# Opening of a two-layer transformer kernel: the modulation's first weights read in column halves

## The reference

```python
def rms_norm(x, g):
    xf = x.astype(jnp.float32)
    y = xf * lax.rsqrt(jnp.mean(xf * xf, axis=-1, keepdims=True) + EPS)
    return (y * g.astype(jnp.float32)).astype(x.dtype)
...
    c_act = jax.nn.silu(c)
    for l in range(DEPTH):
        mods = jnp.split(c_act @ w_ada[l] + b_ada[l], N_MOD, axis=-1)
        sh1, sc1, gt1, sh2, sc2, gt2, sh3, sc3, gt3 = mods

        h = modulate(rms_norm(x, g_ffn1[l]), sh1, sc1)
        x = x + 0.5 * gt1[:, None, :] * swiglu(h, w1_gu[l], w1_down[l])
```

## Time and profile before

| | us |
|---|---|
| median of 3 runs | 2141.09 (2136.44 to 2141.6) |
| the profiled execution's own time | 2139.85 |
| its span, first to last instruction | 2138.1 |
| PE busy | 2077.5 (97%) |
| DVE busy | 1385.1 (65%) |
| ACT busy | 815.6 (38%) |

### The profile page before, as it was taken

How to read it: one execution, slowest core, us unless ns; L and a number is a source line. 1 busy time by engine, 2 the same in 40 slices (tenths; PEclk the granted TensorE clock), 3 DMA queues, 4 the chain that set the end, 5 groups by cost and what they waited for, 6 DMA issues and landing times.

```text
span 2138.1 us, 30256 instructions
## 1 busy us (share of the span) xinstructions
PE 2077.5 (97%) x12206; PEld 1782.2 (83%) x12206; DVE 1385.1 (65%) x1992; ACT 815.6 (38%) x1178; POOL 50.0 (2%) x62
## 2 busy tenths in 40 slices
PE   7999999999999999999999999999999998999998
PEld 6888888788887777889998988777688887989897
DVE  7766665644324774576886777766565467869595
ACT  4222212412332563443342444566443433424243
POOL 2000000000000000000000000000030000000000
PEclk9999999999999999999999999999999999999999
DMA  9554553232222112222232223301133122323322
GB/s 369 216 192 186 196 193 122 80 117 96 99 91 88 40 58 81 79 99 106 91 118 95 102 99 117 140 21 41 43 116 138 40 79 89 111 86 104 113 98 109
DMA packets 36745, 238.36 MB, mean 111 GB/s; under 512 B 4454, under 2 KB 6758, under 8 KB 8872
## 3 DMA queue, kind: packets, MB, share of 16 engines
q1 hardware_dynamic: 35132, 232.10, 29.7%
q10 hardware_dynamic: 1516, 4.94, 0.6%
HBM read 230.73 MB, written 6.29 MB: 111 GB/s over the span
## 4 chain that ended last, share of the span: by engine, by line
PE 85%; DVE 8%; ACT 4%; issue 2%; POOL 1%; DMA 0%; SPq 0%; DVEq 0%; ACTq 0%; POOLq 0%
PE ps L649 84%; PE ps L1075 1%; ACT w_hi L1502 1%; DVE ada_acc L2386 1%; DVE w_lo L2204 1%; DVE w_lo L2562 1%; POOL x L2157 0%; DMA ada_slot<-in_ada 0%; DVE w_lo L2739 0%; ACT square L1502 0%; ACT pt L1502 0%; DVE act_lo L2261 0%; ACT act_hi L1502 0%; ACT normed L1502 0%; DVE normed L2702 0%
## 5 line engine op out<-in xcount | busy, mean ns | idle before, releaser
L649 PE MATMUL ps<-act_hi,w_hi 128*128 128x512 f32 (+1 forms) x1672 | 617.1, 369 | 12.9 <-DVE w_lo L2562 4.6
L649 PE MATMUL ps<-act_hi,w_lo 128*128 128x512 f32 (+1 forms) x1672 | 607.4, 363 | 0.0
L649 PE MATMUL ps<-act_lo,w_hi 128*128 128x512 f32 (+1 forms) x1672 | 607.2, 363 | 0.0
L1502 ACT ACTIVATE w_hi<-raw 128x2048 fp32r<-128x2048 f32 (+4 forms) x205 | 339.2, 1660 | 312.3 <-PE ps L649 295.5
L649 PEld LDWEIGHTS ps<-act_hi,w_hi 128*128 128x128 f32 x1672 | 317.0, 190 | 69.4 <-issue 9.8
L649 PEld LDWEIGHTS ps<-act_hi,w_lo 128*128 128x128 f32 x1672 | 316.9, 190 | 49.7
L649 PEld LDWEIGHTS ps<-act_lo,w_hi 128*128 128x128 f32 x1672 | 317.2, 190 | 47.1 <-issue 1.0
L2204 DVE TENSOR_TENSOR w_lo<-raw,w_hi 128x2048 fp32r<-128x2048 f32 x102 | 234.0, 2294 | 56.2 <-ACT w_hi L1502 54.5
L649 PE MATMUL ps<-hid_hi,w_hi 128*128 128x512 f32 (+1 forms) x680 | 260.7, 383 | 2.8 <-DVE hid_lo L2729 1.7
L649 PE MATMUL ps<-hid_lo,w_hi 128*128 128x512 f32 (+1 forms) x680 | 259.6, 382 | 0.0
L649 PE MATMUL ps<-hid_hi,w_lo 128*128 128x512 f32 (+1 forms) x680 | 259.5, 382 | 0.0
(11 more groups left out here) (419 smaller groups left out, 3177.0 us busy)
## 6 DMA issues: line engine op xcount, KB each, us to landing
raw<-in_weights SPq DMA_DIRECT2D x176, 1024.0 KB, 4.8
ada_raw<-in_ada SPq DMA_DIRECT2D x30, 1024.0 KB, 4.8
ada_slot<-in_ada SPq DMA_DIRECT2D x6, 1024.0 KB, 14.7
bias_rows<-biasrow SPq DMA_DIRECT2D x8, 320.0 KB, 17.2
x<-in_x SPq DMA_DIRECT2D x1, 2048.0 KB, 8.2
table<-bias_rows ACTq DMA_DIRECT2D x1, 2048.0 KB, 8.9
result<-x SPq DMA_DIRECT2D x7, 256.0 KB, 2.2
kept_x<-x ACTq DMA_DIRECT2D x1, 1536.0 KB, 5.1
```

The costliest lines, as they stand in the source:

```text
L649: return nc.tensor.matmul(out, lhsT, rhs, start=start, stop=stop)
L1502: return nc.scalar.activation(out, in_, func, **kw)
```

## The change

The two groups that the first layer needs (scale 1 and shift 0) are read and summed in **halves of 512 columns**: first the columns of features 0 to 511 of group 1, then of group 0, then the columns of features 512 to 1023 in the same order. Each half is 4 loads of 512 KB in rows of 2048 bytes.

- Weight block 0 is loaded right behind `x`, ahead of the modulation; block 1 between the two halves.
- Of each half, input tiles 0 and 1 (half 0) or tile 0 (half 1) are multiplied on PE straight from the loaded weights, one column at a time (`first_products`). DVE sums the other 6 or 7 tiles of 128 x 512, with the running sum in PSUM and the last step into `ada_acc` (`first_sum_of`); PE adds that over the partitions (`first_columns`).
- The first 4 tiles of `act_hi` and `act_lo` are made from half 0, and PE multiplies blocks 0 and 1 by these 4 tiles (`first_half(0, 0)`, `first_half(1, 0)`) before the other 4 tiles of both. Its order is written out: block 0 half 0, then block 1 half 0, columns of half 1, block 0 half 1, block 1 half 1.
- `keep_warm` is gone from the opening. `w_lo` of block 0 is made by POOL instead of DVE.
- The bias rows are made one by one in banks 0 to 3, and ACT copies three of them before `x` is there.
- `ada_step`, on which SP's `next_ada` waits, is raised by 16 at once, with `negsink`, after the last `act_lo` tile.

```diff
+FIRST_ON_PE = ((0, 1), (0,))
+FIRST_DONE, _at = {}, 0
+for _half in range(2):
+    for _g in (1, 0):
+        _at += 8 - len(FIRST_ON_PE[_half])
+        FIRST_DONE[_half, _g] = _at
...
+        halves_of = [buf[:].rearrange("p u (e n) -> p (u e) n", e=2) for buf in ada_raw]
+        first_slots = {(0, 1): (act_slots[0][:], act_slots[2][:]), (0, 0): halves_of,
+                       (1, 1): (act_slots[1][:], act_slots[3][:]), (1, 0): (y[:, 0:4, :], y[:, 4:8, :])}
...
+            def load_first(half, g):
+                cut = slice(half * (D // 2), half * (D // 2) + D // 2)
+                for part in range(2):
+                    for b in range(2):
+                        at = (4 * g + 2 * part + b) * BLOCK
+                        block = ten["ada"][at:at + BLOCK].rearrange("(p u n) -> p u n", p=P, u=2)
+                        sp.dma_start(first_slots[half, g][part][:, 2 * b:2 * b + 2, :],
+                                     block[:, :, cut]).then_inc(ada_first_in[half, g][part], 16)
...
-            load_first(0)
-            load_first(1)
+            load(0, 0)
+            load_first(0, 1)
             sp.dma_start(ident, ten["consts"][:, 0:P]).then_inc(ident_in, 16)
-            for b in range(2, ADA_FIRST):
-                load_first(b)
-            load(0, 0)
+            load_first(0, 0)
             load(0, 1)
+            load_first(1, 1)
+            load_first(1, 0)
...
+            def first_products(half, g, t):
+
+                pe.wait_ge(ada_first_in[half, g][t // 4], 32)
+                for j in range(4):
+                    mm(first_column(half, g, j), first_slots[half, g][t // 4][:, t % 4, j * P:j * P + P],
+                       c_act[:, t:t + 1], False, False)
+
+            def first_columns(half, g):
+
+                pe.wait_ge(first_step, FIRST_DONE[half, g])
+                for j in range(4):
+                    at = 4 * half + j
+                    last = mm(first_column(half, g, j), ada_acc[g][:, at * P:at * P + P], ones[:, 0:1],
+                              False, j == 3)
+                if (half, g) == (1, 0):
+                    last.then_inc(ada_sum, 2)
+                else:
+                    last.then_inc(first_sum, 1)
+
+            def first_half(k, half):
+
+                pe.wait_ge(block_used, k + 1)
+                for t in range(4 * half, 4 * half + 4):
+                    if t < 6:
+                        pe.wait_ge(second_low if k else first_low, t // 2 + 1)
+                    else:
+                        pe.wait_ge(split_lo, k + 1)
+                    pe.wait_ge(act_ready, t + 1)
+                    for u in range(2):
+                        cut = slice(u * P, u * P + P)
+                        out = ps[:, 2 * k + u, :]
+                        mm(out, w_hi[k][:, t, cut], act_hi[:, t, :], t == 0, False)
+                        mm(out, w_hi[k][:, t, cut], act_lo[:, t, :], False, False)
+                        last = mm(out, w_lo[k][:, t, cut], act_hi[:, t, :], False, t == DT - 1)
+                if half:
+                    last.then_inc(block_done, 1)
...
+            pe.wait_ge(c_ready, 1)
+            for g in (1, 0):
+                begin_columns(0, g)
+                for t in FIRST_ON_PE[0]:
+                    first_products(0, g, t)
             begin_stats()
             pe.wait_ge(sq_ready, DT)
             add_columns(square[0])
             add_columns(square[1], stop=True).then_inc(ms_ready, 1)
-            ada_columns(0)
+            first_columns(0, 1)
             pe.wait_ge(ident_in, 16)
             pe.wait_ge(rinv_ready, 1)
             for i in range(NT):
                 last = mm(ps[:, 5, i * P:i * P + P], rinv[:, i:i + 1].to_broadcast([P, P]), ident)
             last.then_inc(rstd_ready, 1)
             norms[0] += 1
-            keep_warm(4 * WARM)
-            ada_columns(1)
-            keep_warm(5 * WARM)
+            first_columns(0, 0)
+            first_half(0, 0)
+            pe.wait_ge(first_mods, 1)
+            for g in (1, 0):
+                begin_columns(1, g)
+                for t in FIRST_ON_PE[1]:
+                    first_products(1, g, t)
+            first_half(1, 0)
+            first_columns(1, 1)
+            first_columns(1, 0)
+            first_half(0, 1)
+            first_half(1, 1)
...
+            for h in range(3):
+                bias_row(h)
             act.wait_ge(x_in, 16)
-            for t in range(3):
+            for t in range(5):
                 squares(t, x[:, t, :])
-            bias_rows(0)
-            squares(3, x[:, 3, :])
-            bias_rows(1)
-            squares(4, x[:, 4, :])
-            bias_rows(2)
+                bias_row(3 + t)
             squares(5, x[:, 5, :])
-            bias_rows(3)
+            act.wait_ge(raw_in[0], 16)
+            first_hi_half(0)
             squares(6, x[:, 6, :])
             squares(7, x[:, 7, :])
+            first_hi_half(1)
...
+            act.wait_ge(first_mods, 1)
+            prenorm(mods[:, 0:8], 0, 4, after=second_hi)
+            second_hi(3)
             act.wait_ge(mods_ready, 1)
-            prenorm(mods[:, 0:8], after=second_hi)
+            prenorm(mods[:, 0:8], 4, DT)
...
+                pool.wait_ge(first_hi if t < 2 else split_hi, 1)
+                pair = slice(2 * t, 2 * t + 2)
+                nc.gpsimd.tensor_tensor(w_lo[0][:, pair, :], raw[0][:, pair, :],
+                                        w_hi[0][:, pair, :].bitcast(F32),
+                                        ALU.subtract).then_inc(first_low if t < 3 else split_lo, 1)
...
+            def first_sum_of(half, g, ts):
+
+                bank = (2, 5)[g] if half == 0 else 4
+                total = ada_acc[g][:, half * (D // 2):half * (D // 2) + D // 2]
+                order = [t for t in range(DT) if t not in FIRST_ON_PE[half]]
+                for t in ts:
+                    at = FIRST_DONE[half, g] - len(order) + order.index(t)
+                    dve.wait_ge(ada_first_in[half, g][t // 4], 32)
+                    out = total if t == order[-1] else ps[:, bank, :]
+                    tile = first_slots[half, g][t // 4][:, t % 4, :]
+                    if at:
+                        dve.wait_ge(first_step, at)
+                    if t == order[0]:
+                        ins = v.tensor_scalar(out, tile, c_act[:, t:t + 1], None, ALU.mult)
                     else:
-                        dve.wait_ge(ada_step, 2 * b + u)
-                        ins = v.scalar_tensor_tensor(out=acc[:], in0=ada_slots[b][:, u, :],
-                                                     scalar=c_act[:, t:t + 1], in1=acc[:],
-                                                     op0=ALU.mult, op1=ALU.add)
-                    ins.then_inc(ada_step, 1)
-
-            def first_low(u):
-
-                dve.wait_ge(split_hi if u else first_hi, 1)
-                half = slice(4 * u, 4 * u + 4)
-                ins = v.tensor_tensor(w_lo[0][:, half, :], raw[0][:, half, :],
-                                      w_hi[0][:, half, :].bitcast(F32), ALU.subtract)
-                if u == 1:
-                    ins.then_inc(split_lo, 1)
+                        ins = v.scalar_tensor_tensor(out=out, in0=tile, scalar=c_act[:, t:t + 1],
+                                                     in1=ps[:, bank, :], op0=ALU.mult, op1=ALU.add)
+                    ins.then_inc(first_step, 1)
...
-            for b in range(6):
-                ada_first_block(b)
+            on_dve = [[t for t in range(DT) if t not in ts] for ts in FIRST_ON_PE]
+            first_sum_of(0, 1, on_dve[0])
+            dve.wait_ge(brow_copied, 8)
+            first_sum_of(0, 0, on_dve[0][:-2])
             norms[0] += 1
             dve.wait_ge(root_ready, 1)
             v.reciprocal(rinv[:, 0:NT], root[:, 0:NT]).then_inc(rinv_ready, 1)
-            ada_first_block(6)
-            ada_first_block(7)
-            first_low(0)
-            modulation(0, 2)
-            gain(0, 1, "g_ffn1").then_inc(mods_ready, 1)
-            v.tensor_scalar(negsink[:], col("sinks", 0, 16), -1.0, None, ALU.mult)
-            dve.wait_ge(mods_ready, 1)
+            first_sum_of(0, 0, on_dve[0][-2:])
+            link(first_modulation(0, 1))
+            first_gain(0)
             dve.wait_ge(rstd_ready, 1)
-            prenorm(gains[:, 0], mods[:, 0:8], begin=lambda: first_low(1))
+            first_gained(0)
+            first_gained(1)
+            first_modulation(0, 0).then_inc(first_mods, 1)
+            first_gained(2)
+            first_act_low(0)
+            first_gained(3)
+            for t in range(1, 4):
+                first_act_low(t)
+            first_sum_of(1, 1, on_dve[1])
+            first_sum_of(1, 0, on_dve[1][:-2])
+            link(first_modulation(1, 1))
+            first_gain(1)
+            first_sum_of(1, 0, on_dve[1][-2:])
+            first_gained(4)
+            first_gained(5)
+            first_modulation(1, 0).then_inc(mods_ready, 1)
+            first_gained(6)
```

(64 more changed lines are left out.)

44 lines of the change are left out of this document (12 added, 32 removed).

## The result

| | before | after |
|---|---|---|
| median of 5 runs each, us | 2136.45 (2136.24 to 2141.6) | 2152.09 (2147.9 to 2152.55) |
| the profiled execution's own time | 2139.85 | 2151.61 |
| its span | 2138.1 | 2149.8 |
| block 2 starts on PE | 65.4 | 76.9 |
| span behind that | 2072.7 | 2072.9 |

The ratio of the mean times is **1.0061, 95% interval 1.0048 to 1.0074**: the change makes the kernel slower by 0.6%. (The medians lie 0.7% apart, since the five times before fall into two groups, near 2136.4 and near 2141.3, and their median is in the lower one.) The last two rows say where: block 2 starts 11.5 us later, and all behind it lasts as long as before. The forecast had +7.5 us for that start.

A forecast was written before the change was run, and what follows sets the result against it. The prediction took PE's back-to-back products from 49 us on as the bound. Late root and reload move block 2's start from 65.4 to 72.9, +7.5 us on 2139.85: 2147.4 us, range 2139.5 to 2153.

The forecast's parts named there:

- a late root: Opening: PE's one-column products come ahead of the statistics, which end at 29.85 us instead of 26.76.
- a late reload: Before block 2: modulation load issued at 61.4 us behind `negsink`, landing at 66.2; block 2 starts at 72.9 instead of 65.4.
- unseen costs: Opening: PSUM sums, clock of first products and load behind `negsink`, together about -3 to +3 us: 2144.5 to 2151.
- rival 3: Opening loads: 0.5 MiB loads don't overlap, 3.6 us each, over 2166 us; slowed by a quarter only, 2150.5; together 13%.
- 1.16 a head: PE's bias rows in the opening: cost as before, 1.16 us a head, ending near 15.7 us.
- a wait for group 0's load: PE, half 0: group 1's tiles fit until 19.2 us, group 0's start with their load at 20.5.
- The clock between one-column products and waits: PE, opening: upper level from 41.5 us, block 1's 24 products done at 52.5, group 1's columns at 53.5.
- The last stretch: Opening's end: last `act_lo` at 61.3 us, then reload, two sums, a product and `w_lo` until block 2 at 72.9.
- (1): PE, opening: one-column products take 0.119 us at the upper level; block 2 at 65.0, 2139.5 us; 12%.
- (2): Before block 2: with rival 1, the reload is also hidden and block 1's end decides, 61.7; 2136.2 us; 3%.
- (4): Before block 2: load lands by 60 us, block 1's end decides, 69.6 to 71.7; 2144 to 2146 us; 10%.

The follow-up runs named there:

- Experiment 3: Changed kernel with bias rows made again by pairs of heads on two PE row groups: block 2's `silu` 2.4 us sooner, at 85.74 us.
- e5: Changed kernel with the modulation reload released early and products of zeros in PE's waits: 2144.77 us, one execution.
- e10: Changed kernel with one edit, POOL's four subtractions for block 1 waiting for the fourth `act_lo`: 2147.85 us, one execution.
- e1: Changed kernel with `negsink` and its `ada_step` increment moved up behind half 0's shift, so the reload is issued early: 2149.28 us, one execution.
- e4: Changed kernel with half 1's group 1 columns moved to the middle of block 1's first half on PE: 2152.94 us, one execution.
- Experiment 9: Changed kernel with half 0's sums on DVE, early reload, zero products, columns amid, POOL's block 1 subtractions later: 2141.33 us median of 10, ratio 1.0006 to before.
- e6: Changed kernel with bias pairs, earlier squares and root, tiles moved, columns amid, early reload, zero products in PE's waits: 2147.66 us median of 7, ratio 1.004 to before.
- e2: Changed kernel with all tile sums on DVE, none of PE's one-column products of `w_ada`: 2140.43 us, one execution.
- e7: Changed kernel with all tile sums on DVE, the same kernel as e2, timed: 2144.77 us median of 10, ratio 1.0025 to before.

## Why the prediction came out as it did

**Sign and mechanism.** Slower by more than 0.3%, by a late root and a late reload, as forecast. The forecast time, 2147.4 us, is 4.2 below the profiled execution's own 2151.61. That lies inside the whole range (2139.5 to 2153), near its end, and above the 2144.5 to 2151 that the forecast's own unseen costs spanned: neither of the two terms that were missed below stood among these costs, and the range held them by the room that rival 3 had given it. In that the forecast was lucky. Of the marks it named: one-column products at 0.222 (forecast 0.222); DVE idle from 26.2 to 33.4 (24.6 to 30.2); a wait for the columns (to 57.8; forecast 53.5); load issued at 65.47 (61.4), DVE waiting for it; PE idle before block 2, which starts at 76.9 (72.9). Each is there, and from the root on each is late by 3 to 4 us.

**The size.** The sum had +7.5 for block 2's start, the profile shows +11.5. The difference arises in two places:

- *The bias stage, term "1.16 a head".* It ended at 19.7, not 15.7. The step that failed divided a row of pairs by four heads, as if overlap were a property of the head. 0.8 of the 4 us went where the forecast had a wait for group 0's load, the rest into the statistics, 33.1 instead of 29.85. Experiment 3 gives the term its price: 2.1 us at the statistics and 2.4 at block 2.
- *The clock between one-column products and waits.* I had let block 1's first half run at the upper level throughout: 5.4 us. It took 7.2 (49.61 to 56.79), with 7 products at 0.43 from 50.95 on. With the late start this makes the columns end at 57.7, 4.2 late. Some of it looks like chance of the execution: e5 and e10 have such slow products there as well, e1, e3 and e4 have none, and in e1, which starts block 0 at the same time within 0.1 us, the columns come 0.85 us sooner. Experiment 5 shows that holding the clock is possible, in the later gaps.

Small terms nearly cancel. The sums cost 0.86 each and not 0.78, 12 of them +1.0; the last two `act_lo` of half 0 took 1.73 each beside POOL and not 1.13, +1.2: in the earlier trace rows an operation that reads PSUM stands ahead of each, here two `act_lo` follow one another. Both lie on DVE, which had to wait for PE anyway (experiment 10). The first half of block 0 took 7.3 us against 7.4 forecast, nine products at the lower level.

**The last stretch** was forecast best: 11.6 us from the last `act_lo` to block 2, measured 11.5 (65.4 to 76.9). That PE's own end of block 1 would be close behind was in the forecast too (69.6, or 71.7 with a clock drop, against 72.9); the clock did drop, and the end came at 76.3 against 76.9. So the reload's lead over that end was 0.6 us, where these ends gave 1.2 to 3.3, and taking it away gains 0.9 (experiment 1); the forecast named the right last bound, with a second one closer behind it than it said.

**The rivals.** (1) One-column products at the upper level: no, 0.222 in both kernels; PE had been busy without a gap since 12.89 when the products at 29.56 still took 3.55. The Trainium skill, "TensorE: Matmul & The Clock Gate", part 1, has the gate open after sustained matmul activity; read as any matmul, that does not fit these rows. (2) needed rival 1, and goes with it. (3) Small loads: they are not slow as a stream. Two stretches of the kernel after:

```profile
24.00:28.00 4.00, 4.00 (x20) 4.00 (x20) 1.54 (x3) 1.50 (x3) 3.60 (x3) 1.00 1.00 388
...
32.00:36.00 4.00, 4.00 (x20) 4.00 (x20) 1.82 (x5) 0.26 (x1) 0.00 (x0) 1.00 1.05 387
```

388 and 387 GB/s, and 385 to 407 in all such stretches from 16 to 36 us, where the earlier trace rows had 420 (later ones mix with the bias writes queued behind): behind the first tile DVE waited for them 1.04 and 0.52 us, in all. The Trainium skill's rule of loads of 1 MiB or more ("DMA: Bandwidth & Descriptors", section "Measured") comes to 3 to 8% here, with sixteen loads of half that size queued back to back. (4) Only the start late: nearly the truth after the fact, since both bounds end within 0.6 us, but in experiments 4 and 10 the reload is the later one by more.

**What the change could give.** Experiment 9, with five mends, comes level with before, and no run beat the kernel before. In it PE and DVE wait for each other and no longer for loads once DVE's sums have begun at 16.3 us; that this chain of hand-overs is the limit is my reading, no run shows it.

## What to carry to other kernels

Before splitting loads so that work can start sooner, ask what the engine that gets the early work already holds: here PE's order held the statistics that all else waited for, and "free" products in front of them cost 5 us. Write down for each resource the release that comes last: a release moved to the end of a stage (here an increment on `negsink`) put a load's whole 4.8 to 6.3 us behind it. Split a gain by what the edit can reach: of experiment 1's 1.9 us only 0.9 was the edit's. And never divide the time of overlapped instructions by their number to price them singly.

## What the runs showed of the hardware

- **PE stayed at its lower level through 16 us of uninterrupted bias rows and one-column products**: 16 one-column instructions still take 3.55 us at 29.56; behind zero products of 128 columns they take 2.10 (e6, 25.73). The granted clock reads 1.00 up to 44 us although the durations show the lower level; so read durations there, not the column.
- **PE's clock drops in one stretch in some executions and not in others**: in block 1's first half the kernel after, e5 and e10 have 7 products at 0.43 us each, e1, e3 and e4 none, and their edits give no reason for it (one execution each).
- **In these rows DVE and POOL slow each other when both DVE inputs are in SBUF, and not when DVE reads PSUM.** `act_lo` takes 0.75 alone, 1.13 beside POOL behind an operation that reads PSUM, and 1.73 where two follow one another; POOL's subtraction of 128x512 takes 1.60 beside `act_lo` (6.41 for 4), 1.25 beside sums that read PSUM (e9, 5.01 for 4). POOL's additions fell from 1.97 to between 1.26 and 1.35, beside sums that read PSUM or an idle DVE. The Trainium skill, "GPSIMD Engine Reference", section "Specifications", says that contention comes with two SBUF inputs of DVE; the rows agree.
- **A load of 1 MiB on an idle queue**, with others issued right behind it, took 4.8, 4.8, 4.9, 5.0, 5.8 and 6.3 us from issue to use (after, e2, e3, e7, e4, e10). Where it is exposed, its scatter comes straight into the mark.
